# Two layers of mixers on one core: the first attention head's queries moved between two chunks of the last gate tile, and the first output tile's split made in two pieces

## The reference

```
proj = h @ w_in                                   # 512 x (256 + 128 + 64 + 2048)
q_c, kv_c, k_r, z = split(proj)                   # z: the gate, 2048 wide
q_c, kv_c = rms_norm(q_c), rms_norm(kv_c)
q = q_c @ w_uq                                    # per head 128 "nope" + 64 "rope" columns
q_rope, k_rope = apply_rope(q_rope), apply_rope(k_r)
q_lat = q_nope @ w_uk                             # per head 128 wide
s = q_lat @ kv_c.T + q_rope @ k_rope.T            # chunk-causal softmax, 4 blocks of 128 queries
o = (softmax(s) @ kv_c) @ w_uv                    # here: softmax(s) @ (kv_c @ w_uv)
y = (o * silu(z)) @ w_out                         # 512 x 2048 @ 2048 x 1024
```

## Time and profile before

| | us |
|---|---|
| median of 3 runs (lowest to highest) | 1437.62 (1435.53 to 1441.57) |
| the profiled execution, device time | 1435.81 |
| its span, first to last instruction | 1434.0 |
| PE busy in the span | 1353.3 (94%) |
| PEld / DVE / ACT / POOL busy | 1142.7 / 888.9 / 581.9 / 320.8 |
| mean granted TensorE clock | 0.984 of full speed |

### The profile page before, as it was taken

One profiled execution on the slowest core, in us unless ns is written; L12 is line 12 of the kernel. 1 busy time (PEld: TensorE's weight loads), 2 busy tenths in 40 slices (PEclk: granted clock), 3 DMA queues, 4 the chain that ended last, 5 costly groups with the idle time before them and its releaser, 6 DMA issues.

```text
span 1434.0 us, 17573 instructions
## 1 busy us (share of the span) xinstructions
PE 1353.3 (94%) x6875; PEld 1142.7 (80%) x6875; DVE 888.9 (62%) x1284; ACT 581.9 (41%) x882; POOL 320.8 (22%) x210
## 2 busy tenths in 40 slices
PE   1999999999999979999999999999999999999997
PEld 1988888688778868887788878888887788888876
DVE  6754534754574548887544677776676667675553
ACT  1422222322344236655322565643342466543441
POOL 0200200245410034464345200001114300011123
PEclk9999999999999989999999899999999999999998
DMA  9443343233143311112234232313223231211201
GB/s 372 166 156 132 133 163 145 88 133 133 59 169 133 110 43 57 67 45 77 89 132 147 74 132 89 104 73 132 89 88 132 95 126 64 83 60 59 88 31 59
DMA packets 30610, 155.14 MB, mean 108 GB/s; under 512 B 3392, under 2 KB 3520, under 8 KB 19264
## 3 DMA queue, kind: packets, MB, share of 16 engines
q1 hardware_dynamic: 30528, 154.03, 29.7%
HBM read 151.92 MB, written 2.10 MB: 107 GB/s over the span
## 4 chain that ended last, share of the span: by engine, by line
PE 77%; DVE 9%; issue 5%; ACT 5%; POOL 1%; DMA 1%; SPq 1%; DVEq 0%; ACTq 0%; POOLq 0%
PE bank L707 23%; PE bank L709 22%; PE bank L708 22%; PE bank L1020 1%; PE bank L801 1%; DMA w_raw<-wt 1%; DVE neg_max L1616 1%; PE bank L1101 1%; ACT pT L1305 1%; ACT w_hi L1145 1%; PE bank L1075 1%; DVE w_lo L1412 1%; PE bank L819 1%; ACT p_even L1296 1%; PE bank L1077 1%
## 5 line engine op out<-in xcount | busy, mean ns | idle before, releaser
L707 PE MATMUL bank<-h_lo,w_hi 128*128 128x512 f32 x1056 | 418.0, 396 | 11.8 <-DVE w_lo L1412 4.1
L709 PE MATMUL bank<-h_hi,w_hi 128*128 128x512 f32 x1056 | 412.1, 390 | 0.0
L708 PE MATMUL bank<-h_hi,w_lo 128*128 128x512 f32 x1056 | 411.6, 390 | 0.0
L1412 DVE TENSOR_TENSOR w_lo<-w_raw,w_hi 128x2048 fp32r<-128x2048 f32 (+2 forms) x94 | 210.7, 2242 | 102.5 <-ACT w_hi L1145 102.2
L707 PEld LDWEIGHTS bank<-h_lo,w_hi 128*128 128x128 f32 x1056 | 198.5, 188 | 59.0 <-DVE w_lo L1412 5.4
L709 PEld LDWEIGHTS bank<-h_hi,w_hi 128*128 128x128 f32 x1056 | 198.5, 188 | 42.2
L708 PEld LDWEIGHTS bank<-h_hi,w_lo 128*128 128x128 f32 x1056 | 198.7, 188 | 39.7 <-issue 0.5
L1145 ACT ACTIVATE w_hi<-w_raw 128x2048 fp32r<-128x2048 f32 (+2 forms) x94 | 173.1, 1841 | 19.4 <-DMA w_raw<-wt 13.1
L1441 DVE SCALAR_TENSOR_TENSOR acc<-ada_raw,cond,acc 128x1024 f32<-128x1024 f32 x70 | 100.3, 1434 | 0.0
L1219 ACT ACTIVATE tmp<-bank 128x512 f32<-128x512 f32 x48 | 28.6, 596 | 138.4 <-PE bank L709 127.4
L1887 POOL TENSOR_SCALAR q_dup<-rot_y 128x512 fp32r<-128x512 f32 x8 | 11.9, 1492 | 318.6 <-DVE rot_y L1452 318.6
(11 more groups left out here) (276 smaller groups left out, 2589.7 us busy)
## 6 DMA issues: line engine op xcount, KB each, us to landing
w_raw<-wt SPq DMA_DIRECT2D x86, 1024.0 KB, 5.8
ada_raw<-adat SPq DMA_DIRECT2D x80, 512.0 KB, 3.7
ada_first<-adat SPq DMA_DIRECT2D x16, 512.0 KB, 10.3
w_raw<-wt SPq DMA_DIRECT2D x8, 640.0 KB, 4.8
x<-xt SPq DMA_DIRECT2D x4, 512.0 KB, 16.6
out<-outf SPq DMA_DIRECT2D x8, 256.0 KB, 2.2
poolw<-poolt SPq DMA_DIRECT2D x1, 1024.0 KB, 5.7
decay<-decayt SPq DMA_DIRECT2D x1, 1024.0 KB, 5.0
```

The costliest lines, as they stand in the source:

```text
L707: pe.matmul(dst, ah, bl, start=start, stop=False, skip_group_check=True)
L708: pe.matmul(dst, al, bh, start=False, stop=False, skip_group_check=True)
L709: return pe.matmul(dst, ah, bh, start=False, stop=stop, skip_group_check=True)
L1412: dve.tensor_tensor(w_lo[T % 2][:, 0:n], w_raw[T % 2][:, 0:n], f(w_hi[T % 2][:, 0:n]), ALU.subtract).then_inc(w_lo_done, 1)
```

## The change

1. A new step `head_entry` stands between the two chunks of the last gate tile (tile 37). In it TensorE makes `head_qr(0)` and `head_q(0)`; ScalarE copies `qr_f`, `qn_hi` and, once VectorE has the turned queries, both halves of `q_rot[0]`; VectorE does all of the rotary work with `rope`, then `qn_lo` and the two low parts of `q_rot[0]`. GpSimd does nothing for pair 0 any more.
2. The step -1 keeps `head_ql(0)`, `ql_hi`, `ql_lo` and the split of tile 39, which on VectorE now comes after `ql_lo`.
3. Tile 46 is split in two pieces: columns 0 to 1280 in step 14 (first on ScalarE, on VectorE behind the first two score maxima), columns 1280 to 2048 at the end of step 15. TensorE waits for the second piece (`uv_lo_done`) before the rest of the first output chunk, and SyncE waits for it before it loads tile 48.
4. The counts of the rotary semaphores are shifted by one pair, and ScalarE waits for `qr_val` (the sum) where it waited for its two parts.

```diff
@@ plan_steps
             chunk("SZ", T, n=2 * i + sub, sub=sub, tmp=False, post=False)
+            if i == 7 and sub == 0:
+                steps.append(dict(op="head_entry"))
@@ which tile a step splits, and how much
-            return head_tile + MH // 2 if t == MH - 1 else None
+            return head_tile + MH // 2 if t == MH - 2 else None
+        def late_columns(t):
+            if t == MH - 1:
+                return head_tile + MH // 2, slice(HEAD_COLS, TILE)
+            return (splits_in(t), slice(D, HEAD_COLS)) if t >= 1 and t % 2 == 1 and splits_in(t) else None
+        def early_columns(T):
+            j = T - head_tile
+            return D if 2 <= j < MH // 2 else HEAD_COLS if j == MH // 2 else cols_of[T]
@@ sync
-                if 2 <= T - 2 - head_tile < MH // 2:
+                if 2 <= T - 2 - head_tile <= MH // 2:
                     sp.wait_ge(uv_lo_done, T - 2 - head_tile - 1)
@@ tensor, OUT chunks
                     first = OUT1_EARLY if kind == "OUT1" and d["n"] == 0 else 0
+                    if first:
+                        pe.wait_ge(uv_lo_done, MH // 2 - 1)
@@ tensor, steps
+                elif op == "head_entry":
+                    head_qr(0)
+                    head_q(0)
...
-                    if ahead:
+                    if ahead and here:
                         head_q(t + 1)
@@ scalar, split_tile
+                elif j == MH // 2:
+                    act.wait_ge(v_full, 2 * (j - 1))
@@ scalar, steps
+                elif op == "head_entry":
+                    act.wait_ge(qr_full, 1)
+                    act.activation(qr_f[:], bank[:, 5, :], ACT.Copy).then_inc(qr_taken, 1)
+                    act.wait_ge(qn_full, 1)
+                    act.activation(qn_hi[:], bank[:, 7, :], ACT.Copy).then_inc(qn_hi_done, 1)
+                    act.wait_ge(qr_val, 1)
+                    for e in range(2):
+                        r = slice(64 * e, 64 * e + 64)
+                        act.activation(q_rot[0][e][r, :], rope_y[r, :], ACT.Copy).then_inc(qr_hi_done, 1)
...
-                    if t < MH - 1 and T is not None:
+                    if T is not None:
                         split_tile(T)
...
-                    if t == -1:
-                        cast_rope(0)
-                    if t == MH - 1:
-                        split_tile(splits_in(t))
+                    if late_columns(t):
+                        split_late(*late_columns(t))
@@ vector, head(t)
-                if T is not None and t < MH - 1:
+                if T is not None and t >= 0:
                     split_tile(T)
...
                 if t == -1:
-                    rope_turned(0)
-                    rope_low(0, 0)
-                    rope_low(0, 1)
+                    split_tile(T)
+                if late_columns(t):
+                    split_late(*late_columns(t))
                 T = splits_in(t - 1) if t >= 0 else None
                 if T is not None and t < MH:
                     ada_piece(T - 1 + 2 * SEC)
-                if t == MH - 1:
-                    split_tile(splits_in(t))
-                    ada_piece(splits_in(t) - 1 + 2 * SEC)
@@ vector, steps
+                elif op == "head_entry":
+                    dve.wait_ge(qr_taken, 1)
+                    rope(qr_f[:], cos1[:], sin1[:], rope_t[:], rope_y[:], 32, qr_val)
+                    dve.wait_ge(qn_hi_done, 1)
+                    dve.tensor_tensor(qn_lo[:], bank[:, 7, :], f(qn_hi[:]), ALU.subtract).then_inc(qn_lo_done, 1)
+                    rope_low(0, 0)
+                    rope_low(0, 1)
```

More of the change, by code:

```diff
@@ L595, in splits_in @@
                 return head_tile + (t + 3) // 2
-            return head_tile + MH // 2 if t == MH - 1 else None
+            return head_tile + MH // 2 if t == MH - 2 else None
[6 more added lines that the diff above has]
+            return D if 2 <= j < MH // 2 else HEAD_COLS if j == MH // 2 else cols_of[T]
         def rope_pair_at(t):
-            j = 0 if t == -1 else t // 2 + 1 if t % 2 == 0 else MH
-            return j if j < MH // 2 else None
+            j = t // 2 + 1
+            return j if t >= 0 and t % 2 == 0 and j < MH // 2 else None
         def scores_at(i):
@@ L1135, in split_tile @@
             def split_tile(T):
-                n = cols_of[T]
+                n = early_columns(T)
                 act.wait_ge(w_landed[T % 2], 16 * (T // 2 + 1))
@@ L1145, in split_tile, with split_late @@
                 act.activation(w_hi[T % 2][:, 0:n], w_raw[T % 2][:, 0:n], ACT.Copy).then_inc(w_hi_done, 1)
-            def split_values(T):
+            def split_late(T, c):
                 act.wait_ge(v_full, 2 * (T - head_tile - 1))
-                act.activation(w_hi[T % 2][:, D:HEAD_COLS], w_raw[T % 2][:, D:HEAD_COLS],
-                               ACT.Copy).then_inc(uv_hi_done, 1)
+                act.activation(w_hi[T % 2][:, c], w_raw[T % 2][:, c], ACT.Copy).then_inc(uv_hi_done, 1)
             def split_heads(d):
@@ L1334, in _ @@
                         act.wait_ge(qr_full, j + 1)
-                        if j >= 1:
-                            act.wait_ge(qr_turned, 4 * j)
-                            act.wait_ge(qr_cos, j)
+                        act.wait_ge(qr_val, j)
                         act.activation(qr_f[:], bank[:, 5, :], ACT.Copy).then_inc(qr_taken, 1)
@@ L1343, in _ @@
                             copy_turned(i)
-                    if ahead:
+                    if ahead and here:
                         act.wait_ge(qn_full, t + 2)
-                        if t >= 0:
-                            act.wait_ge(ql_full, t + 1)
+                        act.wait_ge(ql_full, t + 1)
                         act.activation(qn_hi[:], bank[:, 7, :], ACT.Copy).then_inc(qn_hi_done, 1)
@@ L1363, in _ @@
                         exp(3)
-                    if 1 <= t < MH - 1 and T is not None:
-                        split_values(T)
-                    if t == -1:
-                        cast_rope(0)
-                    if t == MH - 1:
-                        split_tile(splits_in(t))
+                    if late_columns(t):
+                        split_late(*late_columns(t))
                 elif op in ("att_scores", "att_scores2") and d["u"] < SP_PAIRS:
@@ L1408, in split_tile @@
             def split_tile(T):
-                n = D if 2 <= T - head_tile < MH // 2 else cols_of[T]
+                n = early_columns(T)
                 dve.wait_ge(w_hi_done, T + 1)
@@ L1413, in split_tile, with split_late @@
                                   ALU.subtract).then_inc(w_lo_done, 1)
-            def split_values(T):
+            def split_late(T, c):
                 dve.wait_ge(uv_hi_done, T - head_tile - 1)
-                v = slice(D, HEAD_COLS)
-                dve.tensor_tensor(w_lo[T % 2][:, v], w_raw[T % 2][:, v], f(w_hi[T % 2][:, v]),
+                dve.tensor_tensor(w_lo[T % 2][:, c], w_raw[T % 2][:, c], f(w_hi[T % 2][:, c]),
                                   ALU.subtract).then_inc(uv_lo_done, 1)
@@ L1619, in rope_turned @@
             def rope_turned(j):
-                dve.wait_ge(qr_cos, j + 1)
-                dve.wait_ge(qr_turned, 4 * (j + 1))
+                dve.wait_ge(qr_cos, j)
+                dve.wait_ge(qr_turned, 4 * j)
                 dve.tensor_tensor(rope_y[:], rope_y[:], rope_t[:], ALU.add).then_inc(qr_val, 1)
@@ L1632, in head @@
                 T = splits_in(t)
-                odd = (t + 1) // 2 if ahead and t % 2 == 1 else None
+                odd = (t + 1) // 2 if here and ahead and t % 2 == 1 else None
                 if 0 <= t - 2 < MH:
@@ L1976, in _ @@
                             pool.wait_ge(mc_lo_done, t - 1)
-                        if j >= 1:
-                            pool.wait_ge(qr_val, j)
+                        pool.wait_ge(qr_val, j)
                         for i in range(4):
@@ L1981, in _ @@
                             pool.tensor_tensor(rope_t[to, :], qr_f[of, :], sin1[of, :], ALU.mult).then_inc(qr_turned, 1)
-                            pool.wait_ge(qr_turned, 4 * j + i + 1)
+                            pool.wait_ge(qr_turned, 4 * (j - 1) + i + 1)
 def kernel(x, c, positions, ada_w, ada_b, ln_g, ln_b, e_w_in, gmlp_norm_g, gmlp_norm_b, gmlp_ws, gmlp_bs,
```

1 line of the change is left out of this document (removed).

## The result

| | before | after |
|---|---|---|
| median (lowest to highest), 9 runs each | 1438.02 (1435.05 to 1442.37) | 1428.74 (1427.04 to 1432.28) |
| ratio, with 95% interval | | 0.9941 (0.9925 to 0.9957) |
| profiled execution, device time; span | 1435.81; 1434.0 | 1432.28; 1430.5 |
| mean granted TensorE clock | 0.984 | 0.983 |

The changed kernel is 9.3 us faster by the medians, and the ratio's interval is 6.2 to 10.8 us. The forecast was 1426.5 in a range of 1422.5 to 1431.5. Its profiled execution is the slowest of its nine, so the two profiled times, 3.5 us apart, are a poor pair: stages have to be compared, not spans.

A forecast was written before the change was run, and what follows sets the result against it. TensorE, 77% of the chain, bounds the kernel where it waits or its clock is low. Entry 6.8 + exit 3.2 = 10.0 us off 1435.81 or 1437.62 gives 1425.8 or 1427.6; forecast 1426.5 between them, range 1422.5 to 1431.5.

The forecast's parts named there:

- Queries one chunk earlier, rotary work on VectorE: Entry: query matmuls start 5.4 us earlier, at 504.0; VectorE's rotary products take 4.2 us, `qn_lo` has 1.1 us to spare.
- ScalarE late next: Entry: in-order ScalarE does read-out, tile 39's split, then `ql_hi`; scores start at 515.4 instead of 521.22, 5.8 us earlier.
- The upper end of the entry, 8.5 us: Entry: earlier scores and full clock, less a 0.25 us wait and with ScalarE's copies in line, give 8.5 us.
- One clock fall at the entry, 1.7 us: Entry: the new 2.4 us idle stretch brings one clock fall costing 1.7 us, leaving 6.8; bounds 8.5 and 5.1.
- Head 14 costs nothing: Head 14: VectorE's 1.49 us subtraction of tile 46's first piece fits its 2.29 us idle time; at worst 1.2 us late.
- Exit 3.2 us: Exit: third output product starts at 696.2 instead of 699.40, 3.2 us, including 1.7 of low clock; bounds 1.5 and 3.5.
- The shift is kept: After the entry and exit: heads are paced by their own chain and output tiles keep TensorE full, so gains last.
- (a): Entry: the clock doesn't fall; 8.5 + 3.2 = 11.7 us gained, 1424.1; chance 0.32.
- (b): Entry: VectorE's rotary chain replaces the removed wait, taking 8.3 us; 6.4 us gained in all, 1429.4; chance 0.07.
- (c): Exit: gives nothing, since VectorE reaches `o_taken` no earlier; 6.8 us gained, 1429.0; chance 0.04.
- (d): Before the end: a load or GpSimd's sums in the output tiles absorb the shift; no change, 1435.8; chance 0.04.
- (e): Heads: shifted steps lose the clock once each, 14 x 1.7 = 23.8 us slower, 1449.6; chance 0.03.

The follow-up runs named there:

- e7: ScalarE's copy `ql_hi` put ahead of its split of tile 39, against the changed kernel; 1428.78, ratio 0.9939.
- e2: The exit edit alone (tile 46 split in two pieces) with the entry of before, against before; 1436.60, ratio 0.9986.
- e1: The entry edit alone, tile 46 split whole at the end of step 15, against before; 1431.81 against 1438.66, ratio 0.9956.
- e4: The kernel before with 13 and 17 unused matmuls filling TensorE's two entry waits, against before; 1436.36, ratio 0.9979.
- e5: The changed kernel again, word for word, against before; 1427.88 against 1436.66, ratio 0.9934.
- e6: The changed kernel with the new step's four sine products back on GpSimd; 1433.61, ratio 0.9974.

## Why the prediction was right

The time lies in the range, 2.2 us above the forecast of 1426.5. By the steps of the prediction:

- **Queries one chunk earlier, rotary work on VectorE.** Right: 4.2 us for the six rotary instructions, `qn_lo` with 1.1 us to spare, no wait of `head_ql(0)`.
- **ScalarE late next.** Right: scores 3.2 us behind the last gate chunk were expected, 3.41 came; e7 shows that the split ahead of `ql_hi` is the cause. Its price was taken as 0.9 and measured 1.10; the wait of `head_qr(1)` that takes its place (0.66) is what the prediction would have had to subtract from that gain.
- **The upper end of the entry, 8.5 us.** Right against the traced execution of before, where the clock stays after: 33.88 - 25.5 = 8.4. But 2.9 of these are that execution's own fall; against e2's old entry it is 32.55 - 25.5 = 7.0, and the waits alone are 5.5.
- **One clock fall at the entry, 1.7 us.** The term that was mis-sized, twice over. A fall here is not an expected certainty: one of five traces has it. And when it came it cost 2.7, not 1.7, for it lasted 6.25 us of busy time and not the 3.35 taken over from the exit; the entry of before, with 6.18 in the earlier trace rows, was the nearer row. Weighted by how often it came, it costs 2.7 / 5 = 0.5. The row of 3.40 idle us at a clock of 1.00 didn't bound it either: in e2 the clock fell inside that same wait. Against the traced execution of before the entry thus gives 5.7 or 8.4 us, not 6.8.
- **Head 14 costs nothing.** Right, heads within 0.02 us of each other in before and after. The Trainium skill's rule (SBUF — State Buffer, Who interferes with whom) would have had the subtraction wait for GpSimd's cast. It started at 673.41 inside the cast that ran 672.57 to 674.06 and took its plain 1.48, so the trace doesn't agree. The one that grew is GpSimd's own subtraction, which started inside VectorE's: 1.89 to 1.90 in every trace with the split in head 14 and 1.29 to 1.30 in e1 and e4 without it. That is 0.60 us more for the 0.75 in which the two ran together.
- **Exit 3.2 us.** Right: 3.10, and the parts too (expected 1.75 for the first product, 1.8 for `o_taken`, 1.8 for tile 48's load; measured 1.72, 1.88, 1.83). The clock's share of it, which was put at 1.7, is 3.10 - 1.89 = 1.2 and not always there to gain: e1's old exit kept the clock, and then the split is worth 1.9.
- **The shift is kept.** Right to the last output tile: the stretches from the third output product to the last agree within 0.03 us in all kernels. After it the tail varies from 645.8 to 650.3, roughly with its time at half clock, 29 to 41 us. e4, which changes only the filling of the old entry, has 650.1: the tail of the one profiled execution of before was the shortest of the twelve. So against before's trace the stages give 5.69 + 3.10 = 8.8 with the fall and 8.4 + 3.1 = 11.5 without it, while the medians say 9.3 and 8.8 in the two sets (0.9941 and 0.9934). The rest is before's trace, which lost the clock at both places and at the entry for longer than e2's. An estimate without it: waits of 5.5 and 1.9, together 7.4; and the mean granted clock over all executions, which rose by 0.002 (from 0.9841 in 13 of before to 0.9860 in e5's 5), at 0.5 to 1.0 us for each 0.001 (see the last section) 1 to 2 more. That is 8.4 to 9.4. Whether the falls in the tail follow from the shift or come as they like is open: there is no second trace of before.
- **Luck in the number.** Two errors of the sum lay against each other. It charged the new entry 1.7 us for a fall that one trace in five has, and it credited the change with both old falls in full, 3.1 and 1.7, as the one traced execution showed them, where e2's old entry lost 1.5 and e1's old exit nothing.

The rivals: (a), no fall at the entry, is what four of five traces show, and I gave it less than the forecast; its time of 1424.1 was still too low, since it was counted from one execution of before, with an unusually short tail and with the clock lost at both places. The Trainium skill (TensorE: Matmul & The Clock Gate, What's actually happening) calls the number of slow matmuls in one kernel run-variable. The five traces agree: 6.8 us at half clock in one, none in four. (b) fell: the rotary chain takes the place of the wait only on GpSimd, as e6 shows. (c) fell with e2's 1.9 to 3.1 us in the trace. (d) fell: no load or sum before the last output tile takes the shift back. (e) fell: the heads keep their clock in every trace.

## What to carry to other kernels

Where TensorE waits at a seam between two stages, look for a unit of the earlier stage behind which the first operands of the next can be made; then price what stands next in each in-order queue, for taking away the wait of 4.50 us uncovered 2.56, and taking 1.10 of that uncovered 0.66. Move four small products from GpSimd to VectorE where VectorE is idle. A clock fall read off one trace is a chance and not a cost, in the old kernel as in the new one: give it a share on both sides, take its length from the nearest stage, and compare stages, not spans.

## What the runs showed of the hardware

- Whether the clock falls in one and the same gap of 2.56 us differs from one execution to the next (1 of 5 here), and so does the place: in the old entry it fell at 517.4 in before and at 514.9 in e2. Over the 28 runs of before in the first set the time rises by some 1.0 us for each 0.001 of mean granted clock that is lost, and the clock goes from 0.979 to 0.986: most of the kernel's scatter. Over the 13 of the second set the slope is only 0.5.
- Of two subtractions that overlap for 0.75 us in head 14, GpSimd's, the later one, stretched from 1.30 to 1.90 us, while VectorE's kept 1.48. GpSimd's cast, inside which VectorE's started, kept 1.49.
- A 32-row product of 512 columns takes GpSimd 1.28 us by itself and 1.47 in a row of four, and VectorE 0.68, which is what 128 rows take VectorE.
